# Delta rule: the state's decay as one VectorE instruction behind the new values, the update as another

## The reference

```python
def step(S, xs):
    qc, kc, uc, wc, gcc, ac = xs
    v_new = uc - jnp.einsum('bhck,bhkv->bhcv', wc, S)
    o = (jnp.einsum('bhck,bhkv->bhcv', qc * jnp.exp(gcc)[..., None], S)
         + jnp.einsum('bhij,bhjv->bhiv', ac, v_new))
    g_last = gcc[..., -1]
    S = (S * jnp.exp(g_last)[..., None, None]
         + jnp.einsum('bhck,bhcv->bhkv', kc * jnp.exp(g_last[..., None] - gcc)[..., None], v_new))
    return S, o
```

## Time and profile before

| | |
|---|---|
| median of 3 runs | 1598.96 us (1595.99 to 1602.51) |
| the profiled execution's own time | 1603.34 us |
| its span in the trace | 1601.6 us |
| PE busy | 1566.0 us (98%) |
| DVE busy | 647.4 us (40%), 1210 instructions |
| ACT busy | 568.2 us (35%) |
| POOL busy | 618.9 us (39%) |

### The profile page before, as it was taken

One profiled execution on the slowest core, in us unless ns is written; L12 is line 12 of the kernel. 1 busy time (PEld: TensorE's weight loads), 2 busy tenths in 40 slices (PEclk: granted clock), 3 DMA queues, 4 the chain that ended last, 5 costly groups with the idle time before them and its releaser, 6 DMA issues.

```text
span 1601.6 us, 31800 instructions
## 1 busy us (share of the span) xinstructions
PE 1566.0 (98%) x13520; PEld 1511.3 (94%) x13520; DVE 647.4 (40%) x1210; ACT 568.2 (35%) x999; POOL 618.9 (39%) x513
## 2 busy tenths in 40 slices
PE   8999999999999999999999999999999999999998
PEld 7999987888998999999999998699999999999998
DVE  4484145454435522322223534844263223232244
ACT  5133264334435421312223322854364223131232
POOL 3754201113561453444444442035424444443441
PEclk9999998999999999999999999999999999999999
DMA  5222211003241223222322223013403223223221
GB/s 149 94 81 81 81 56 60 3 2 119 80 158 51 83 79 96 89 80 84 101 80 90 96 79 133 16 54 104 134 30 98 85 80 105 81 79 106 79 80 56
DMA packets 123061, 131.85 MB, mean 82 GB/s; under 512 B 6285, under 2 KB 115122, under 8 KB 122930
## 3 DMA queue, kind: packets, MB, share of 16 engines
q1 hardware_dynamic: 118128, 125.24, 24.2%
q10 hardware_dynamic: 4802, 4.66, 0.9%
HBM read 122.44 MB, written 7.45 MB: 81 GB/s over the span
## 4 chain that ended last, share of the span: by engine, by line
PE 48%; issue 31%; POOL 17%; DVE 2%; ACT 1%; DMA 1%; POOLq 0%; ACTq 0%; DVEq 0%
PE LP L832 38%; POOL wl L723 17%; PE LP L1222 3%; PE MP L988 1%; PE LP L937 1%; DMA stage<-in_w_in_ab 1%; PE MP L961 0%; PE LP L1164 0%; PE MP L1062 0%; PE MP L1222 0%; PE MP L1206 0%; PE MP L1198 0%; PE MP L1079 0%; PE MP L1314 0%; PE MP L1309 0%
## 5 line engine op out<-in xcount | busy, mean ns | idle before, releaser
L723 POOL TENSOR_TENSOR wl<-stage,wh 128x512 fp32r<-128x512 f32 x428 | 578.7, 1386 | 798.6 <-ACT wh L1599 786.2
L832 PE MATMUL LP<-xh,wh 128*128 128x272 f32 x2112 | 440.9, 290 | 4.9 <-DVE xl L2160 3.9
L832 PE MATMUL LP<-xh,wl 128*128 128x272 f32 x2112 | 437.7, 289 | 0.0
L832 PE MATMUL LP<-xl,wh 128*128 128x272 f32 x2112 | 436.1, 288 | 0.0
L1599 ACT CAST wh<-stage 128x2048 fp32r<-128x2048 f32 x107 | 204.0, 1906 | 441.9 <-PE LP L832 414.7
L832 PEld LDWEIGHTS LP<-xh,wh 128*128 128x128 f32 x2112 | 332.7, 189 | 7.4 <-DVE xl L2160 5.2
L832 PEld LDWEIGHTS LP<-xl,wh 128*128 128x128 f32 x2112 | 332.3, 189 | 0.0
L832 PEld LDWEIGHTS LP<-xh,wl 128*128 128x128 f32 x2112 | 330.5, 189 | 0.0
L832 PE MATMUL LP<-hh,wh 128*128 128x272 f32 x1024 | 211.3, 287 | 0.0
L832 PE MATMUL LP<-hh,wl 128*128 128x272 f32 x1024 | 210.5, 288 | 0.0
L832 PE MATMUL LP<-hl,wh 128*128 128x272 f32 x1024 | 210.3, 287 | 0.0
(11 more groups left out here) (419 smaller groups left out, 1671.2 us busy)
## 6 DMA issues: line engine op xcount, KB each, us to landing
stage<-in_w_up SPq DMA_DIRECT2D x32, 1024.0 KB, 5.4
stage<-in_w_down SPq DMA_DIRECT2D x32, 1024.0 KB, 5.2
stage<-in_w_in_ab SPq DMA_DIRECT2D x13, 1024.0 KB, 5.3
stage<-in_w_xkv SPq DMA_DIRECT2D x8, 1024.0 KB, 5.2
stage<-in_w_in_c SPq DMA_DIRECT2D x6, 1024.0 KB, 5.0
stage<-in_w_out_ab SPq DMA_DIRECT2D x4, 1024.0 KB, 10.7
stage<-in_w_xq SPq DMA_DIRECT2D x4, 1024.0 KB, 5.3
stage<-in_w_xo SPq DMA_DIRECT2D x4, 1024.0 KB, 5.1
```

The lines of the kernel that those rows point to most:

```text
L723: pool.tensor_tensor(wl[s][:, part], stage[s][:, part], wh[s][:, part].bitcast(f32), ALU.subtract).then_inc(w_lo, 1)
L832: mm = pe.matmul(LP[:, 2 * slot + half, 0:b - a], weights, X[part][k][:, a:b], start=(first and n_ == 0), stop=(last and n_ == 2), skip_gr ...
```

## The change

Behind `vnew`, one DVE instruction now multiplies the old state of all four heads by the decay (the factor `eg` is repeated over 128 columns) and writes it to the buffer of the new state. It counts on a new semaphore, `decayed`. When PE's product is there, one DVE instruction adds it to that buffer. The four instructions that did both per head go.

```diff
+        decayed = sem("decayed")
...
                     dve.tensor_tensor(vnew[p, :, :], um[j][p, :, :],
                                       state_bank(c)[p, :].rearrange("p (h n) -> p h n", h=H),
                                       ALU.subtract).then_inc(rec_dve, 1)
+                    decay_ = eg[:, j, c, :].rearrange("p (h o) -> p h o", o=1).to_broadcast([128, H, 128])
+                    dve.tensor_tensor(S[:, new, :, :], S[:, old, :, :], decay_, ALU.mult).then_inc(decayed, 1)
                 elif name == "ds":
                     dve.wait_ge(rec_pe, 3 * q + 2)
-                    for h in range(H):
-                        inst = dve.scalar_tensor_tensor(out=S[:, new, h, :], in0=S[:, old, h, :],
-                                                        scalar=eg[:, j, c, h:h + 1],
-                                                        in1=MP[:, 2, 128 * h:128 * h + 128], op0=ALU.mult, op1=ALU.add)
-                    inst.then_inc(rec_dve, 1)
+                    dve.wait_ge(decayed, q + 1)
+                    dve.tensor_tensor(S[:, new, :, :], S[:, new, :, :],
+                                      MP[:, 2, :].rearrange("p (h n) -> p h n", h=H), ALU.add).then_inc(rec_dve, 1)
```

## The result

The changed kernel is slightly slower: 1602.55 us (median of 22 runs, 1597.74 to 1610.06) against 1600.20 us (22 runs, 1595.99 to 1604.8). The ratio is 1.0018, 95% interval 1.0009 to 1.0026. That is 2.9 us of 1600, between 1.4 and 4.2, so inside the 0.5% that were called the same.

What follows compares the result with a forecast made beforehand. PE, busy 1566.0 of 1601.6 us, was taken as the bound, with DVE mattering only where PE stands still in the delta rule. Chunk shifts summed to +0.9 us, taking 1598.96 to 1599.9 us; range 1595 to 1604.

Steps and rivals of the forecast that it cites:

- rival 2: In q4 to q6 DVE and POOL hold each other up and PE's clock falls once more: 1603.4 us; chance 0.15.
- Prices of decay and add: The two new DVE instructions in each chunk: about 0.69 us each, taken as 0.66 in the queue.
- q2: Chunk q2: `z` sooner behind the shorter state, -0.2 us; POOL slipping between decay and `mul` was the bound +0.4.
- q4: Chunk q4: DVE without a gap from `vnew` to `z`, so `z`, ACT and PE come 0.28 us later; bounds +0.16, +0.4.
- q5 and q6: `lo` delays POOL's pieces and PE's projection, +0.5 us; decay and `mul` taking turns with POOL delay PE's transposition, +0.5.
- q8: Behind chunk q8: `z` and last norm sooner, -0.2 us; last `mul` ahead of POOL could win up to 0.8; bounds -1.0, +0.3.
- Sum: Shifts of PE over all nine chunks: -0.2 + 0.28 + 0.5 + 0.5 - 0.2 = +0.9 us.
- Rival 1: All nine chunks gain the 0.43 us of the shorter state: 3.9 us, 1595.1 us; chance 0.1.
- The rule on the DRAIN: Skill's rule that the next VectorE instruction waits for an empty pipe: four per-head instructions 1.37 us; forecast followed the row, 1.12.
- The signs named beforehand: Among them: no PE wait for the state in q5, `vnew` to `z` in q4 about 3.5 us, DVE about 2.3 us busier.
- signs of being wrong: PE waiting for decay or add, clock falls in other places, or the delta-rule stretch changing by more than 3 us.
- theory B: Formed after the measurement: PE's longer pauses let its clock fall more often, though not in every execution; 1.7 to 3.4 us each.

Runs made afterwards that it cites:

- late: Changed kernel with the decay moved behind the displaced instructions, directly ahead of the wait for PE's product; ratio to the kernel before 1.0011.
- only56: Kernel before with the new decay and add in chunks q5 and q6 alone, four per-head instructions in the other seven; ratio 1.0007.
- extra_sbuf: Kernel before plus the decay instruction (two SBUF inputs) behind `vnew` in all nine chunks, its result overwritten; ratio 1.0039.
- fill_q2: Changed kernel with 4 unused matmuls on PE in chunk q2 alone, ahead of the transposition that waits for `mul`; ratio 1.0007.
- no_pool: Changed kernel with the old per-head form back in chunks q2, q5 and q6, where POOL works at the same time; 1599.89 us, ratio 0.9992.
- busy_before: Kernel before with unused matmuls in PE's pauses: 8 in q6, 4 each ahead of the transpositions of the sample's and tile 1's output; ratio 1.0010.
- fill_before: Kernel before with 4 unused matmuls on PE in q2 and 4 in q6; 1597.52 us, ratio 0.9981.
- extra_psum: Kernel before plus one DVE instruction behind `vnew` with one PSUM and one SBUF input, 64 partitions, result overwritten; ratio 1.0009.
- best: Changed kernel with the old form in q2, q5 and q6, plus 4 unused matmuls in q2 and 4 in q6; 1598.71 us, ratio 0.9991.
- changed, again: The changed kernel run and profiled once more without any edit; 1602.55 us, ratio to the kernel before 1.0020.

## Why the prediction was right or wrong

It was right that the time would stay within 0.5%, and 1602.55 lies within 1595 to 1604. The mechanism of the point forecast (+0.9 us, from waits alone) is not what was measured: 2.9 us is above even the 2.7 that all its upper bounds together gave, and what came was rival 2, to which I had given 0.15. The range holds the result only because its upper end was that rival's 1603.4. Point by point:

- **Prices of decay and add** (0.69 each): 679 and 687 ns. Right.
- **q2**, forecast -0.2, bounds -0.3 and +0.4: +0.20. POOL did slip in between decay and `mul`, the case that I had as the bound.
- **q4**, +0.28: +0.11. DVE has no gap there as read, but decay to `mul` is 0.61 us and add to `z` 0.59, nearer to 0.6 than to the 0.66 that I took for all.
- **q5 and q6**, +1.0 together: +0.59 from `vnew` of q5 to `vnew` of q7. POOL's pieces did delay PE's first projection part, by 0.31 us and not 0.5; that the shorter state of q5 would make the pause longer from its other side, by 0.27, I had seen but not counted as a risk for the clock. The wait for `mul` was 0.21 and not 0.5.
- **q8**, -0.2, bounds -1.0 and +0.3: -0.91. The last `mul` came in ahead of POOL and took 0.69 us instead of 1.47, and PE's wait for it is gone. The case was named, but as the bound.
- **Sum**, +0.9: -0.01 in the profile whose clock falls are those of before. The measured +2.9 us are thus not explained by the terms of the sum.
- **The step that was mis-sized** is the one that puts no further falls of the clock into the forecast and leaves them to rival 2, with 0.15. By the mean clocks (0.9931 against 0.9947) they are 1.8 to 2.6 of the 3.3 us between the mean times. Six fillers in q6 bring the clock back to 0.9945 and the ratio from 1.0018 to 0.9991, 4.3 us, where in the profile at an equal clock they change nothing. Rival 2 had the mechanism and the place; its price of 1.7 us a fall was low for the falls seen behind q6, which cost 10.20 - 7.35 = 2.9 us in one profile and 3.8 in another. Its row on q4 was a weak one: that window ends 0.5 us behind the pause at 351.51 (the clock did stay at 1.00 in the next one, 352 to 358 us).
- **Rival 1** (the shorter state carries through, 3.9 us): refuted; q5 to q6 gained 0.27, and in the other stretches no gain can be put down to the state; the 0.91 us behind q8 are for 0.78 the shorter `mul`.
- **The rule on the DRAIN**: that four per-head instructions take 1.12 us, not 1.37, held in every profile with the old form. I had quoted the Trainium skill, VectorE: DVE Perf Modes, by half, though: its section on the DRAIN also says that a next instruction that is not held starts earlier, and the rows show that case (a start every 0.26 us at 342 ns each), so they don't contradict it.
- **The signs named beforehand**: PE's matmuls did not wait for the add in q5, as forecast, and `vnew` to `z` of q4 grew, but to 3.31 us and not 3.5; DVE works 3.2 us more, not 2.3. But two of the signs of being wrong came: the clock fell in another place (behind q6), and in the first profile the stretch changed by 4.16 us, more than the 3 allowed; in the second by -0.01.

Open is how often the clock falls, and whether the longer pause is what brings it down: that is argued from the runs with fillers. Of the six profiles with the pause of some 1.3 to 1.5 us in q6 left unfilled (both of the changed kernel, late, only56, extra_sbuf, fill_q2) three have a fall behind it; of six with at most 0.94 us (before, no_pool, busy_before, fill_before, extra_psum, best) three have one in q5 or q6 too, two of them short. So single profiles don't prove theory B; the mean clocks of the timed executions and the runs with fillers carry it. Also open is why 4.3 us (by the intervals 1 to 7) came off when the two falls seen there cost 2.9 and 3.8, not every execution has one, and the clock regained (0.0014) is worth only 1.6 to 2.3 by the same estimate.

## What to carry to other kernels

Fewer instructions on an engine that is not the bound gain nothing; ask what stands next in its queue and who waits for that. An elementwise VectorE instruction with two SBUF inputs put beside GpSimd work costs more than its own time: compare the chunks with and without GpSimd work before placing it. When a change moves time between engines by tenths of a microsecond, look at TensorE's pauses too, since behind a pause 0.6 us longer a fall of the clock cost 2.9 and 3.8 us here, where there was one, and a handful of unused matmuls in the pause is a cheap test, with the same fillers in the kernel before as its control. The mean granted clock of all timed executions tells more than the falls in one profile.

## What the hardware showed that I had not expected

- Who comes first between DVE and POOL is decided by tenths: the same `mul` took 0.69 us with the changed kernel and 1.47 before, and 1.67 in extra_sbuf.
- A fall of the clock behind a pause of 1.5 us cost 3.8 us in fill_q2, and the same program (changed, again) had a fall there in one execution and none in the next.
- Eight unused matmuls (1597.52 us against 1600.35) gained more than any form of the state update. They are eight more than the kernel has already.
